# Prompt window attention in a two-layer streaming encoder step: one query tile a step, and two

## What is computed

```python
def _softmax_with_sink(scores, sink):
    s = jnp.broadcast_to(sink.astype(jnp.float32)[:, :, None, None], scores.shape[:-1] + (1,))
    p = jax.nn.softmax(jnp.concatenate([scores, s], axis=-1), axis=-1)
    return p[..., :-1]

def _window_attend_prompt(q, k, v, sink):
    ...
    scores = jnp.einsum('bcqkgd,bcskd->bckgqs', qc, kb).astype(jnp.float32) * SCALE
    scores = jnp.where(valid, scores, NEG_INF)
    p = _softmax_with_sink(scores, sink.reshape(A_KV_HEADS, A_GROUP))
    out = jnp.einsum('bckgqs,bcskd->bcqkgd', p.astype(v.dtype), vb)
```

## Time and profile before

| | us |
|---|---|
| median of three timed runs | 3590.11 |
| lowest and highest of them | 3585.29, 3593.44 |
| profiled execution, own time | 3591.6 |
| profiled execution, span | 3589.7 |
| stage `pa`, first DMA issue to first DMA issue of the next stage | 275.53 to 375.92 |

### The profile page before, as it was taken

The page is one execution under the profiler, slowest core; times in us unless marked ns, Lnnn a source line. Parts: engine busy times, 40 slices in busy tenths (PEclk is TensorE's granted clock), DMA queues, the critical chain, the costliest instruction groups (busy, mean ns, idle before and its releaser), DMA issues. The chain is left out here.

```text
span 3589.7 us, 62098 instructions
## 1 busy us (share of the span) xinstructions
PE 3324.9 (93%) x24520; PEld 2904.6 (81%) x24520; DVE 1594.3 (44%) x2913; ACT 1123.3 (31%) x2343; POOL 252.5 (7%) x338
## 2 busy tenths in 40 slices
PE   8997699798999999998899889999898999999998
PEld 7886477577999999997789866667677999999997
DVE  5427477463333333335231167777543333333335
ACT  4215255443212112113222155555533121111211
POOL 2310000032000000003000000000022000000003
PEclk9999699899999999999899989999999999999999
DMA  5436599533111111112554399999553111111103
GB/s 174 124 126 188 154 368 331 182 136 117 35 35 58 35 47 35 35 45 89 145 170 138 117 346 337 332 333 341 207 182 112 41 35 35 58 38 44 35 23 112
DMA packets 398381, 493.16 MB, mean 137 GB/s; under 512 B 68464, under 2 KB 250256, under 8 KB 398032
## 3 DMA queue, kind: packets, MB, share of 16 engines
q1 hardware_dynamic: 398176, 490.35, 41.2%
HBM read 407.10 MB, written 84.10 MB: 137 GB/s over the span
## 5 line engine op out<-in xcount | busy, mean ns | idle before, releaser
L2597 DVE TENSOR_TENSOR f_gated<-f_gated,f_up 128x384 f32<-128x384 f32 x132 | 73.1, 554 | 706.3 <-ACT f_gated L2488 706.3
L2620 DVE TENSOR_TENSOR f_y<-f_y,f_down 128x512 f32<-128x512 f32 x396 | 269.9, 686 | 234.3 <-PE f_down L2787 234.3
L2762 PE MATMUL f_gate<-m_ht_hi,f_w_hi 128*128 128x384 f32 x1056 | 355.1, 336 | 12.0 <-DVE f_w_lo L2647 12.0
L2762 PE MATMUL f_gate<-m_ht_hi,f_w_lo 128*128 128x384 f32 x1056 | 354.6, 336 | 0.0
L2762 PE MATMUL f_gate<-m_ht_lo,f_w_hi 128*128 128x384 f32 x1056 | 354.6, 336 | 0.0
L2762 PE MATMUL f_up<-m_ht_hi,f_w_lo 128*128 128x384 f32 x1056 | 352.8, 334 | 0.0
L2762 PE MATMUL f_up<-m_ht_lo,f_w_hi 128*128 128x384 f32 x1056 | 352.8, 334 | 0.0
L2762 PE MATMUL f_up<-m_ht_hi,f_w_hi 128*128 128x384 f32 x1056 | 352.8, 334 | 0.0
L2787 PE MATMUL f_down<-f_wo_hi,f_act_hi 128*128 128x512 f32 x792 | 312.6, 395 | 9.6 <-DVE f_y L2620 5.2
L2787 PE MATMUL f_down<-f_wo_lo,f_act_hi 128*128 128x512 f32 x792 | 309.8, 391 | 0.0
L2787 PE MATMUL f_down<-f_wo_hi,f_act_lo 128*128 128x512 f32 x792 | 309.7, 391 | 0.0
(11 more groups left out here) (410 smaller groups left out, 6744.6 us busy)
## 6 DMA issues: line engine op xcount, KB each, us to landing
jc_kc<-in_cache_c_k SPq DMA_DIRECT2D x64, 1024.0 KB, 11.0
jc_vc<-in_cache_c_v SPq DMA_DIRECT2D x64, 1024.0 KB, 8.2
jb_kc<-in_cache_b_k SPq DMA_DIRECT2D x32, 1024.0 KB, 11.6
jb_vc<-in_cache_b_v SPq DMA_DIRECT2D x32, 1024.0 KB, 8.1
m_raw<-in_w_ffn_in SPq DMA_DIRECT2D x44, 512.0 KB
f_raw<-in_w_ffn_in SPq DMA_DIRECT2D x44, 512.0 KB
f_raw_o<-in_w_ffn_out SPq DMA_DIRECT2D x22, 1024.0 KB, 6.4
m_raw<-x SPq DMA_DIRECT2D x18, 512.0 KB, 4.1
```

The costliest lines, as they stand in the source:

```text
L2597: dve.tensor_tensor(prod[:, b], silu[:, b], up[:, bank, 0:gw], ALU.mult).then_inc(prod_done, 1)
L2620: dve.tensor_tensor(part, part, down[:, half, :], ALU.add).then_inc(added, 1)
L2762: last = pe.matmul(acc[:, bank, 0:gw], a[:, s, k, u, :], b[:, k, token], start=(k == 0 and j == 0), stop=(k == KT - 1 and j == 2))
```

## The change

`prompt_attention` goes, and `window_attention` takes its place. A step is now a pair: one head and two neighbouring query tiles, 32 pairs in all, tiles in rising order. Two pairs make a quad. PE and DVE in the steady state:

- `scores` has four buffers of [2, 256], one PSUM bank each, so score(p+4) waits for the exponentials of pair p. Both tiles of a pair have 256 columns, tile 0 too: its left half gets a constant of -1e30 by one more identity matmul (`closed`).
- One DVE reduction takes the maxima of both tiles, and one instruction joins the sink for both.
- ACT takes two exponentials a pair without accumulator read, and one exponential of the sink for a quad.
- The values have a 65th column of ones, so that `attend` gives the row total in column 64 (matmuls of 65 columns).
- One copy of up to 512 columns moves the four transposes of a pair, on DVE for even pairs, on ACT for odd ones.
- `output` runs once a quad: one addition of 4 totals and 4 sinks, one reciprocal of 4, one product of 256 columns.
- Keys and values of a key/value head are loaded once for its four query heads. The first loads are the first halves (512 frames) of the first keys and queries, then the sinks, the values, and the second halves; then three whole heads of queries, and the second keys and values.
- A store takes two heads (128 columns), and there are 4 where there were 8.

The diff, cut to the parts that the steps below speak of:

```diff
-                sp.dma_start(k_both[:, e].bitcast(F32), paired(planes, k, DH, True)).then_inc(qk_loaded[e], 16)
-                sp.dma_start(q_hi[:, e].bitcast(F32), paired(planes, q, DH, False)).then_inc(qk_loaded[e], 16)
-                sp.dma_start(q_lo[:, e].bitcast(F32), paired(planes[1:2], q, DH, False)).then_inc(qk_loaded[e], 16)
-            def load(i, e):
-                sp.dma_start(v[:, e], y[0:PROMPT, bass.ds(v_cols(i, e), dv)].rearrange(
...
-                act.activation(probs[:, j % 4, 0:count[t] * P], scores[:, j % 2, 0:count[t] * P], ACT.Exp,
-                               bias=neg_top[:, j % 4:j % 4 + 1],
-                               accum_out=total[:, j % 4:j % 4 + 1]).then_inc(exp_done, 1)
-                if sinks is not None:
-                    act.activation(sink_exp[:, j % 4:j % 4 + 1], sink[:, e:e + 1], ACT.Exp,
-                                   bias=neg_top[:, j % 4:j % 4 + 1]).then_inc(sink_exp_done, 1)
...
-                    dve.tensor_scalar(dst, src, inv_j, None, ALU.mult).then_inc(out_done, 1)
...
+        scores = st.ps("scores", [P, 4, 2, 2 * P])
...
+            early, late, whole = slice(0, half), slice(half, PROMPT), slice(0, PROMPT)
+            load_k(0, early, first_loaded)
+            load_q(0, early, first_loaded)
+            sp.dma_start(sink[:], rows(sinks)).then_inc(sink_loaded, 16)
+            load_v(0)
+            load_k(0, late, k_loaded[0])
+            load_q(0, late, q_loaded[0])
+            load_q(1, whole, q_loaded[1])
+            load_q(2, whole, q_loaded[2])
+            load_q(3, whole, q_loaded[3])
+            load_k(1, whole, k_loaded[1])
+            load_v(1)
+            for h in range(4, A_Q):
+                sp.wait_ge(scores_done, per_head * (h - 3))
+                load_q(h, whole, q_loaded[h % 4])
+                if h % 2 == 1:
+                    store((h - 5) // 2)
+            store(2)
+            store(3)
+            for g in range(2):
+                sp.wait_ge(stored[g], 32)
...
+            pool.memset(v[:, :, :, DH:DH + 1], 1.0).then_inc(setup, 1)
...
+                if p >= 4:
+                    pe.wait_ge(exp_done, 2 * (p - 3))
+                for e in range(2):
+                    t = tile(p, e)
+                    query, dst = slice(t * P, (t + 1) * P), scores[:, p % 4, e]
+                    if t == 0:
+                        pe.matmul(dst[:, 0:P], ident_b[:], closed[:], start=True, stop=True)
+                    a = P if t == 0 else 0
+                    key = slice((t - 1) * P + a, (t + 1) * P)
+                    pe.matmul(dst[:, a:], q_hi[:, h % 4, query], k_both[:, kv, key], start=True, stop=False)
+                    pe.matmul(dst[:, a:], q_lo[:, h % 4, query], k_both[:, kv, key], start=False, stop=False)
+                    last = pe.matmul(dst[:, a:], ident_b[:], mask[:, a:], start=False, stop=True)
+                last.then_inc(scores_done, 1)
+            def turn(p):
+                if p >= pairs:
+                    return
+                if p >= 2:
+                    pe.wait_ge(copied[p % 2], p // 2)
+                for e in range(2):
+                    pe.wait_ge(exp_done, 2 * p + e + 1)
+                    for x in range(2):
+                        if tile(p, e) + x >= 1:
+                            last = pe.transpose(turned[:, p % 2, 2 * e + x], probs[:, p % 4, e, x * P:(x + 1) * P], ident[:])
+                last.then_inc(turned_done, 1)
+            def attend(p):
+                q, kv = p // 2, head(p) // A_GROUP
+                if p % (per_head * A_GROUP) == 0:
+                    pe.wait_ge(v_loaded[kv], 16)
+                pe.wait_ge(copied[p % 2], p // 2 + 1)
+                if q >= 2 and p % 2 == 0:
+                    pe.wait_ge(out_done, q - 1)
+                for e in range(2):
+                    t = tile(p, e)
+                    for x in range(2):
+                        if t + x >= 1:
+                            last = pe.matmul(sums(q)[:, 2 * (p % 2) + e], probs_t[:, p % 4, 2 * e + x], v[:, kv, t - 1 + x],
+                                             start=(x == 0 or t == 0), stop=(x == 1))
+                last.then_inc(pv_done, 1)
...
+            for p in range(pairs):
+                score(p + 3)
+                turn(p + 1)
+                attend(p)
...
+                    act.activation(probs[:, p % 4, e], scores[:, p % 4, e], ACT.Exp,
+                                   bias=neg_top[:, p // 2 % 4, 2 * (p % 2) + e:2 * (p % 2) + e + 1]).then_inc(exp_done, 1)
...
+            exponential(0)
+            exponential(1)
+            exponential_sink(0)
+            for p in range(pairs):
+                exponential(p + 2)
+                if p % 2 == 0:
+                    copy_turned(act, p + 1)
+                else:
+                    exponential_sink(p // 2 + 1)
...
+                dve.wait_ge(scores_done, p + 1)
+                dve.tensor_reduce(top[:, p % 4], scores[:, p % 4], AX.X, ALU.max, negate=True).then_inc(top_done, 1)
+                dve.wait_ge(top_done, p + 1)
+                dve.tensor_scalar(neg_top[:, q % 4, 2 * (p % 2):2 * (p % 2) + 2], top[:, p % 4], neg_sink[:, h:h + 1], None,
+                                  ALU.min).then_inc(neg_done, 1)
+            def output(q):
+                h, two = head(2 * q), head(2 * q) // 2
+                dve.wait_ge(sink_done, q + 1)
+                dve.wait_ge(pv_done, 2 * q + 2)
+                dve.tensor_tensor(total[:, q % 2], sums(q)[:, :, DH], sink_exp[:, q % 2], ALU.add).then_inc(total_done, 1)
+                dve.wait_ge(total_done, q + 1)
+                dve.reciprocal(inv[:, q % 2], total[:, q % 2]).then_inc(inv_done, 1)
+                dve.wait_ge(inv_done, q + 1)
+                if q % 4 == 0 and two >= 2:
+                    dve.wait_ge(stored[two % 2], 16)
+                first = q % 2 * 4
+                dve.tensor_tensor(out[:, two % 2, first:first + 4, h % 2 * DH:(h % 2 + 1) * DH], sums(q)[:, :, 0:DH],
+                                  strided(inv[:, q % 2], 0, [1, 4], [0, DH]), ALU.mult).then_inc(out_done, 1)
...
+            for p in range(pairs):
+                if p % 2 == 0 and p:
+                    output(p // 2 - 1)
+                maximum(p + 3)
+                if p % 2 == 1 and p + 1 < pairs:
+                    copy_turned(dve, p + 1)
+            output(quads - 1)
```

More of the change, by code:

```diff
@@ L2949, in build @@
     project_ab(nc, "abp", x0, gain(0, 0), a["w_ab_in"][0], a["rope_table"], planes_ab[0], planes_ab[1], qs_ab, v_ab, k_rows_out, v_rows_out, direct)
-    prompt_attention(nc, "pa", A_Q // 2, lambda i, e: (2 * i + e) * DH, lambda i, e: D + (i // 2) * DH,
-                     lambda i, e: (i // 2) * DH, lambda i, e: (2 * i + e) * DH, planes_ab, v_ab, o_ab, DH,
-                     window=True, sinks=a["a_sinks"])
+    window_attention(nc, "pa", planes_ab, D, v_ab[0:PROMPT], a["a_sinks"], o_ab)
     sample_window(nc, "sa", qs_ab, by_stream(a["cache_a_k"]), by_stream(a["cache_a_v"]), ka_new,
```

409 lines of the change are left out of this document (124 added, 285 removed).

## The result

| | before | after |
|---|---|---|
| median of four timed runs, us | 3591.78 | 3565.66 |
| lowest, highest | 3585.29, 3593.91 | 3563.42, 3567.86 |
| profiled execution, own time | 3591.6 | 3567.86 |
| stage `pa`, to the next stage's first DMA | 275.53 to 375.92 | 275.53 to 354.10 |

The ratio is 0.9934, 95% interval 0.9921 to 0.9946: 26.1 us less at the medians, where 20 were forecast (3570; range 3562 to 3582). Two single executions further down, one of DVE by tile and one of the kernel before, took over 8350 us and are left out of the ratios.

What follows compares the result with a forecast made beforehand. DVE was taken to bound the kernel at 1.325 us a unit, then PE at 1.02 a tile. PE's work, start, clock and end put the next stage at 355.0, 20.9 us earlier than 375.92: 3570 from 3591.6, range 3562 to 3582.

Steps and rivals of the forecast that it cites:

- DVE bounds before, PE after: Stage's steady state: DVE sets the pace before at 1.325 us a unit; PE becomes the bound at 1.02 a tile.
- DVE's price: DVE's work in the changed kernel: 3.22 us for a quad of four tiles, 0.81 a tile.
- Rival 2: DVE stays the bound because strided instructions cost more; at 5.0 us a quad it gives 3584; chance 0.08.
- PE's price: PE's work: 1.02 us a tile for 56 tiles, 0.69 for each of 8 tiles 0, in all 62.6 us.
- Rivals 1 and 4: 1: PE slower, 1.12 us a unit, 3576, chance 0.20. 4: PE faster, DVE bounds at 0.81, 3555, chance 0.05.
- Rival 3: 65-column value product loses its overlap through its odd width: 0.168 us on each of 240 records, 3610; chance 0.05.
- The start: First loads: early scores near 281, then a gap; continuous work near 284.8 plus 0.5 us for slower value loads.
- scores done ahead: Scores of four tiles run during the loading, gaining 4 x 0.36 = 1.44 us of PE's work.
- The clock: PE at half pace until 292, so 6.7 us hold 3.35 of full-clock work; bounds 3.35 us either way.
- The end: After PE's last work: stall 0.3 us, last output 0.73, hand-over 0.2, then 3.5 plus 0.5 to the next stage.
- The stage's sum: Next stage starts at 355.0 and not at 375.92, 20.9 us earlier.
- The rest of the 26.1: Program behind two barriers: the change can only move the moment at which the next stage begins.

Runs made afterwards that it cites:

- DVE by tile: Kernel after, with DVE's maxima and outputs taken one tile at a time again: stage 100.5 us, whole 3589.25 us, ratio to before 1.0001.
- maxima by tile: Kernel after, with only the maxima taken one tile at a time (two reductions, two minima a pair): stage 80.3 us, whole 3566.67, ratio 0.9935.
- without low part and mask: Kernel after, without the matmul of the queries' low part and without the mask's matmul: stage 66.5 us, whole 3551.47.
- 64 columns: Kernel after with 64 columns of values instead of 65, no column of ones, value rows 256 B apart: stage 80.4 us.
- two buffers: Kernel after with two score buffers instead of four: stage 79.3 us, whole 3566.79, ratio 0.9938.
- after again: Kernel after, unchanged, run again on the same chip as its two GpSimd variants: stage 78.9 us, whole 3564.85, ratio 0.9937.
- before with four buffers: Kernel before with four score buffers instead of two, all else as it was: stage 99.9 us, ratio 0.9987.
- whole first: Kernel after, first keys and queries loaded whole instead of in halves, no wait at score(2): stage 78.2 us, whole 3560.57, ratio 0.9934.
- without the low part: Kernel after without the matmul of the queries' low part (64 matrices left out): stage 71.8 us, whole 3553.87.
- corners on GpSimd: Kernel after, mask's matmul replaced by GpSimd memsets of masked corners: whole 3554.69, ratio 0.9908; second version, first keys and queries also loaded whole: 3555.18, 0.9907.

## Why the prediction was right

- *DVE bounds before, PE after.* Shown: with DVE by tile all of the 26 us are gone; maxima by tile leave the 7.89 us a head as they are; a matrix less gives 0.118 us a tile. (In the prediction's count of DVE's instructions before, six of the eleven work on a single column, not five; nothing hangs on it.)
- *DVE's price*, 3.22 us a quad: the rows after sum to 2 x 0.687 + 2 x 0.228 + 0.619 (mean of 0.686 and 0.552) + 0.154 + 0.178 + 0.424 = 3.21; by start distances, without low part and mask, it is about 3.0. Rival 2 is out.
- *PE's price*: 7.89 us a head against 7.83. Rivals 1 and 4 are out (rival 1's 1.12 us a unit stands in none of the rows shown). Rival 3 fell with the 64 columns. The Trainium skill's page "TensorE: Matmul & The Clock Gate", section "Back-to-back issue gap", gives about 81 ns for a matmul of 128 columns with its weight load, sustained. The trace after does not agree for these float32 products: eight records of L945 took 0.90 us (326.67 to 327.57), 0.11 each, as before.
- *The start*: first scores at 281.2 and a pause to 285.6, as forecast (281, 285.3). The 1.44 us for scores done ahead hold against the kernel before, as the sum below shows. What the prediction did not see is another way to the same gain: with the first keys and queries loaded whole ahead of the values, continuous work begins 2 us earlier, and the halves are worth only 0.4 us more than that.
- *The clock*: 288.9 for 292, worth 1.6 us, within the 3.4 allowed. Over the kernels here it rose 11.1 to 16.6 us after the stage's start. Since PE does half of its pace until then, a stage with the same work ends later by half of what its continuous work begins later and half of what the clock rises later. For two buffers, 64 columns and after again this gives 0.75, 0.72 and 0.38 us more than after; their last outputs end 0.72, 0.72 and 0.36 us later, counted from the stage's start.
- *The end*: no stall of 0.3 us showed at the last pair. From the last output's end (349.84) to the next stage it took 4.26 us, against 4.0.
- *The stage's sum*: 354.10 for 355.0, 21.8 us saved for 20.9. Put together from what was measured: 8 x 7.89 - 1.44 = 61.7 us of PE's work at full clock, of which 288.9 - 285.6 = 3.3 us at half pace hold 1.7; 288.9 + 60.0 = 348.9, and the last product ends at 348.91 by the profile (346.95 + 1.96, a modelled end). So the terms are right in kind. That the sum is within 1 us is in part luck: the clock (1.6 too late) and the stall (0.3) were taken too long, the pace (0.5 over eight heads), the start (0.1) and the end (0.3) too short.
- *The rest of the 26.1* lies behind the barrier, where the prediction had put nothing. The sample window took 35.2 us instead of 37.8 in the two profiles. Two windows of 5 us with its value products, before and after, at the same distance (about 20 us) from its start, show another granted clock (the third number from the end, 0.50 and 0.84), and more matmuls done with it (17 and 25):

```profile
395.92:400.92 5.00, 5.00 (x17) 3.58 (x16) 0.00 (x0) 1.06 (x2) 0.00 (x0) 0.50 0.00 0
```

```profile
374.10:379.10 5.00, 5.00 (x25) 3.55 (x23) 0.84 (x2) 1.11 (x3) 0.00 (x0) 0.84 0.00 0
```

Is that the change's doing? The three profiles with a stage of 100 us (before, DVE by tile, before with four buffers) have 37.7 to 37.8; of the six with 78 to 81 us (after twice, maxima by tile, two buffers, 64 columns, whole first) four have 34.6 to 35.2 and two 37.9 and 37.4; the four with 66 to 74 us (without the low part, without mask too, corners on GpSimd twice) have 34.6, 35.8, 33.0 and 33.0. What goes with it in all thirteen is whether the clock rises to 1.00 again some 20 to 25 us into the sample window: it does in the eight with 35.8 us or less and does not in the five with 37.4 or more. A shorter stage before it seems to favour that; no run here shows why, and I leave open whether it is the change's doing. The last 1 to 2 us are within the spread of four runs a side.

## What to carry to other kernels

When two engines look equally full, ask which waits for the other, and read start distances at a place without waits: the second engine's distance is what the change can reach at most, and here it gave the saving of the stage within 1 us, with errors that partly cancelled. Between variants of one kernel, compare such a distance too and not the length of the stage, which the clock's moment moves by more than a us. An engine that works on single columns is relieved by doing several tiles in one instruction; the time an instruction of one column takes (0.15 to 0.21 us) is nearly that of one over four. Once the bound has moved, the next saving is on the new engine: a matmul that only adds a mask went to idle GpSimd for 6 us of the stage.

## What the runs showed of the hardware

- An odd width (65 columns) and rows 260 B apart cost a float32 product nothing: 268 ns and 30.3 us for both widths, and 7.89 us a head.
- A DVE product of 256 columns with strided PSUM input and a scalar repeated over 64 columns costs 0.424 us, about what the plain one did (0.419).
- Two exponentials of 0.47 us take 0.84 in a row of the timeline of after, so the second starts after 0.37. Before, the accumulator read started 0.38 us after the exponential (319.76, 320.14) and lasted 0.19, and the next exponential started 0.09 behind it (320.23): by start distances the read added about 0.1 us.
- The same kernel's clock rose 13.4 and 14.7 us after the stage's start in two executions. Half of that difference, 0.65 us, is stage time where PE bounds; the second stage was 0.35 longer, since its continuous work began 0.55 us earlier (9.48 against 10.03), which gives 0.3 back.
